# Shifting the matmul activations by 32 bytes and the arena by 96 bytes against the weights in SBUF

## The reference, cut to what matters

```python
# first block, layer 0 ("a" stages) and layer 1 ("m" stages)
hn = rms_norm(x, norm_mix[i]);  mix = even_mixer(...) or odd_mixer(...)   # @ w_in, attention, @ w_out
x = x + mix
x = x + sqrelu_mlp(rms_norm(x, norm_mlp[i]), mlp_w1[i], mlp_w2[i])        # 1024 -> 4096 -> 1024
# second block ("r" stages, then "f" stages)
proj = rms_norm_2(x) @ w_in                       # 1024 -> 7698: RNN branch, q, k, v, gates
merged = sigmoid(g_a) * (y_a @ w_proj_a) + sigmoid(g_b) * (y_b @ w_proj_b)
x = x + rms_norm_2(merged @ w_out)
up = causal_dwconv(rms_norm_2(x) @ w_up)          # 1024 -> 6144
x = x + rms_norm_2((gelu(gate) * val) @ w_down)   # 3072 -> 1024
```

## Time and profile before

| what | value |
|---|---|
| three timed runs | 1129.11, 1130.38, 1136.15 us (median 1130.38) |
| the profiled execution | 1134.4 us, its span 1132.6 us |
| TensorE matmul busy | 98% of the span |
| VectorE, ScalarE, GpSimd busy | 69%, 52%, 12% |
| mean granted TensorE clock | 0.995 |

### The profile page before, as it was taken

The page is one execution under the profiler, slowest core; times in us unless marked ns, Lnnn a source line. Parts: engine busy times, 40 slices in busy tenths (PEclk is TensorE's granted clock), DMA queues, the critical chain, the costliest instruction groups (busy, mean ns, idle before and its releaser), DMA issues.

```text
span 1132.6 us, 21593 instructions
## 1 busy us (share of the span) xinstructions
PE 1109.1 (98%) x9351; PEld 1068.6 (94%) x9351; DVE 786.1 (69%) x1134; ACT 587.8 (52%) x828; POOL 140.6 (12%) x109
## 2 busy tenths in 40 slices
PE   7999899999999999999999999999999989999998
PEld 6988799999999999999999997999988989999998
DVE  6567488784457566977644689786475889888752
ACT  4477655443336555544433566854366647666531
POOL 4200050001230005000122206201010000111000
PEclk9999999999999999999999999999999999999999
DMA  9943055566654444555555472666464545556551
GB/s 280 276 150 112 1 184 189 186 195 201 200 187 155 154 139 150 186 187 187 186 187 186 132 212 69 200 200 217 131 221 143 188 147 187 186 187 205 186 184 40
DMA packets 195938, 195.72 MB, mean 173 GB/s; under 512 B 9803, under 2 KB 193028, under 8 KB 195844
## 3 DMA queue, kind: packets, MB, share of 16 engines
q1 hardware_dynamic: 193680, 190.53, 52.9%
q10 hardware_dynamic: 2164, 3.82, 1.1%
HBM read 192.86 MB, written 1.47 MB: 172 GB/s over the span
## 4 chain that ended last, share of the span: by engine, by line
PE 94%; DVE 3%; ACT 2%; DMA 0%; issue 0%; DVEq 0%; SPq 0%; ACTq 0%
PE ps_gemm L1727 50%; PE ps_trans L1727 35%; PE ps_score L1804 2%; PE ps_out L1836 2%; PE ps_trans L1821 2%; DVE act_lo L1144 2%; DVE w_lo L1138 1%; PE ps_gemm L1908 1%; PE ps_score L2035 1%; DMA x_in<-in_x 0%; PE ps_out L2035 0%; PE ps_out L2039 0%; PE ps_score L2039 0%; DVE rs L1150 0%; PE ps_score L1770 0%; ACT prob L798 0%
## 5 line engine op out<-in xcount | busy, mean ns | idle before, releaser
L1138 DVE TENSOR_TENSOR w_lo<-raw,w_hi 128x2048 fp32r<-128x2048 f32 (+2 forms) x179 | 408.2, 2289 | 45.2 <-ACT w_hi L753 45.0
L753 ACT ACTIVATE w_hi<-raw 128x2048 fp32r<-128x2048 f32 (+2 forms) x179 | 332.3, 1863 | 175.2 <-DMA raw<-in_mlp_w 95.3
L1727 PE MATMUL ps_gemm<-act_hi,w_hi 128*128 128x256 f32 (+1 forms) x960 | 267.1, 286 | 4.7 <-ACT act_hi L1064 4.4
L1727 PE MATMUL ps_gemm<-act_hi,w_lo 128*128 128x256 f32 (+1 forms) x960 | 259.9, 282 | 0.0
L1727 PE MATMUL ps_gemm<-act_lo,w_hi 128*128 128x256 f32 (+1 forms) x960 | 254.8, 281 | 0.5 <-DVE act_lo L1144 0.4
L1727 PE MATMUL ps_trans<-act_hi,w_hi 128*128 128x256 f32 x688 | 193.1, 281 | 1.9 <-DVE w_lo L1138 1.9
L1727 PE MATMUL ps_trans<-act_hi,w_lo 128*128 128x256 f32 x688 | 193.0, 281 | 0.0
L1727 PE MATMUL ps_trans<-act_lo,w_hi 128*128 128x256 f32 x688 | 192.9, 280 | 0.0
L1727 PEld LDWEIGHTS ps_gemm<-act_hi,w_hi 128*128 128x128 f32 (+1 forms) x960 | 182.1, 192 | 10.2 <-issue 8.2
L1727 PEld LDWEIGHTS ps_gemm<-act_hi,w_lo 128*128 128x128 f32 (+1 forms) x960 | 178.6, 190 | 0.3
L1727 PEld LDWEIGHTS ps_gemm<-act_lo,w_hi 128*128 128x128 f32 (+1 forms) x960 | 173.7, 186 | 2.1 <-DVE act_lo L1144 0.9
(11 more groups left out here) (379 smaller groups left out, 2238.9 us busy)
## 6 DMA issues: line engine op xcount, KB each, us to landing
raw<-in_mlp_w SPq DMA_DIRECT2D x64, 1024.0 KB, 5.4
raw<-in_w_in SPq DMA_DIRECT2D x30, 1024.0 KB, 5.4
raw<-in_w_up SPq DMA_DIRECT2D x24, 1024.0 KB, 5.2
raw<-in_od_w_in SPq DMA_DIRECT2D x12, 1024.0 KB, 5.1
raw<-in_w_down SPq DMA_DIRECT2D x12, 1024.0 KB, 5.2
raw<-in_ev_w_in SPq DMA_DIRECT2D x9, 1024.0 KB, 8.1
raw<-in_w_proj_a SPq DMA_DIRECT2D x8, 640.0 KB, 4.3
raw<-in_ev_w_out SPq DMA_DIRECT2D x4, 1024.0 KB, 5.1
```

The costliest lines, as they stand in the source:

```text
L753: act.activation(w_hi[:, slot, 0:k, 0:n], raw[:, slot, 0:k, 0:n], ACT.Copy).then_inc(hi_done, 1)
L1138: dve.tensor_tensor(w_lo[:, slot, 0:k, 0:n], raw[:, slot, 0:k, 0:n], w_hi[:, slot, 0:k, 0:n].bitcast(F32), ALU.subtract).then_inc(w_ready, 1)
L1727: ins = pe.matmul(dst, lhs, rhs, start=(first and opens and opening), stop=(last and closes and i + 1 == len(order)), skip_group_check=True)
```

## The change

The bytes between `conv_f` and `act_hi` grow by 32, and those between `tmp0`'s 8 KB and the arena by another 64. So `act_hi`, `act_lo` and the scratch stretch begin 32 bytes further on (at 96 modulo 128), the arena and all in it 96 bytes further on (at 32 modulo 128). `raw`, `w_lo`, `w_hi`, `x` and the small tiles stay. No instruction is added, removed or moved; only addresses differ. The last tile still ends inside the partition (the assertion leaves 832 bytes).

```diff
     fw = place("conv_f", [P, 4, 2 * NH2])
+    top[0] += 32
     act_hi = place("act_hi", [P, NX, T], F32R)
     act_lo = place("act_lo", [P, NX, T], F32R)
     tmp0 = top[0]
-    arena = tmp0 + 8 * K
+    arena = tmp0 + 8 * K + 64
     assert arena + 70 * K <= 229344, arena + 70 * K
```

## The result

The changed kernel takes 1149.37 us (median of four runs, 1147.65 to 1151.06) against 1131.94 us (four runs, 1129.11 to 1136.15): 1.0146 times as long, 95% interval 1.0108 to 1.0183. The profiled execution takes 1151.06 us, its span 1149.3 us, against 1134.4 and 1132.6 us. So the loss to be explained in the trace is 16.7 us of span.

What follows compares the result with a forecast made beforehand. The prediction took TensorE's matmul count times start-to-start distance as the bound. Its VectorE, ScalarE, DMA and TensorE terms summed to 0 against the profiled 1134.4 us; expecting a median amid earlier runs, it forecast 1131 us, range 1112 to 1148.

Steps and rivals of the forecast that it cites:

- What bounds the kernel: Whole kernel: TensorE is busy 98% of the span, so time is the number of matmuls times their start-to-start distance.
- VectorE, ScalarE, DMA, 0 us: Reads and transfers at shifted addresses cost 0 us; bounds 0.3 us for VectorE and DMA, at most 1.1 us for ScalarE.
- TensorE, 0 us: All matmuls: 0 us, since residues 0 and 64 modulo 128 gave the same two cadences for moving and stationary sides.
- The second argument: Weight load doesn't set the matmul cadence: with 16 stationary columns, ten starts lie in 1.14 us, 114 ns apart.
- rival 1: Matmuls: shifting moving against stationary reads stops the slow cadence forming; 20.9 us less, 1113.5 us; chance 0.17.
- The bounds of that term: TensorE: -20.9 us if the slow cadence goes, +16 us if 8,400 matmuls each open one more piece of memory (1.9 ns).
- Rival 2: Matmuls of line 1727: every restart falls into the slow cadence, 4.45 ns each; 15.6 us more, 1150 us; chance 0.12.
- Rival 3: Matmuls: one more memory piece per operand on top of either cadence, up to 1.9 ns each; 1145 us; chance 0.07.
- Rival 4: Some 8,200 matmuls: the excess over 106.7 ns of columns goes altogether, 75 us less; 1059 us; chance 0.03.
- Rival 5: Placement: the change doesn't do what it says; 1131 us; chance 0.01.
- The lottery: Dense matmuls: each run draws its mix of fast and slow cadences anew, so the median should be 1131 us, some 4 either side.
- The 109.2 ns: Skill's rule for 256 columns: columns over 2.4 GHz plus about 2.5 ns; over some 8,200 dense matmuls, 55 us less.

Runs made afterwards that it cites:

- the scan: Kernel before with weight slots (one kernel) or hidden-layer quarters (three) at varied distances (moving less stationary operand's start): single executions, 1150.44, 1140.24, 1135.74, 1140.12 us.
- distance 0: Kernel before with activations and arena 64 bytes on, weights unmoved, so moving and stationary operands start at the same residue: 1166.43 us, ratio 1.0296.
- the run on columns: Against the kernel with distance 0: matmuls in `f_up` load only 96, 64 or 16 of 128 stationary columns; single execution, 1158.96 us.
- distance 112: Against the kernel before: weights 16 bytes on, activations and arena 192, so moving activations start 112 past the weights modulo 256: 1162.09 us, ratio 1.0247.

## Why the prediction was wrong, point by point

The forecast was 1131 us, the result 1149.4 us: above the range's upper end of 1148 and 1.5% slower.

**What bounds the kernel: right.** TensorE's start-to-start distance is the time. The distances from each matmul of `gemm` to the next matmul add up to 1010.4 us after and 993.7 us before, a difference of 16.7 us, the whole change of the span.

**VectorE, ScalarE, DMA, 0 us: right.** Lines 1637 and 1091 stand within 2 ns of the earlier trace rows in their medians, busy times within 1.3 us of the earlier trace rows, and the 1 MB loads of `raw` from `in_w_in` land in 5.5 us and `x_in` in 4.4 us, against 5.4 and 4.3 in the earlier trace rows.

**TensorE, 0 us: the step that failed.** The prediction took 0, "the nearest rows being those where a shift of 64 bytes between the two sides changed nothing". It measured +15.4 us. Those rows compare distances -64 and +64, and the scan shows these to be the two places, half a period apart, where the two cadences of 113.3 and 117.8 ns live. They look alike because of that, and say nothing of -32 and +32. I had seen one value of a variable twice and read it as two values without a difference. The second argument, that the weight load doesn't set the cadence since 16 stationary columns run at 114 ns, rests on one slab: at distance 0 that slab stays at 113.5 ns while all with 128 columns take 120.0, so the number of stationary columns does count. And the same trace held the third level that rival 1's "against" denies: its slab with 24 columns ran at 116.7 ns (the lines stand with the run on columns).

**The bounds of that term** were -20.9 and +16 us, and the measured 15.4 lies inside, close to the upper one; but they were bounds for other mechanisms, and distance 0 went to some 33 us. Near as the 1.9 ns a matmul of the upper bound and the measured 1.88 are, that is luck too: no dense run before showed it. The true upper end could not be had from the trace, which held no dense run at another distance.

**Rival 1 (the slow cadence can't form any more)** named the likeliest mechanism (argued, not shown), moving and stationary reads meeting, and the means, a shift of one against the other. It had the sign wrong: the shift removed both cadences, the fast one too, and the two that came are at 116.7 and 118.3 ns. It had 0.17; its mechanism with a sign left open deserved more.

**Rival 2 (every restart into the slow cadence)** gave 1150 us and the result is 1149.4, but not by its mechanism. It wanted 11.31 per 96 everywhere; the chain has 11.36 and 11.20 and no 11.31. The times agree since 4,944 + 576 matmuls lie 0.5 ns above the slow cadence and 2,880 lie 1.1 ns below it. Its place (the matmul's line) was right; that its time came out is luck.

**Rival 3 (one piece more on top of either cadence)** is out: after the change each stage has one value, not two raised ones. **Rival 4** is out, no run went below 113.3 ns. **Rival 5** is out.

**The lottery: right for the kernel before, wrong for the changed one.** The kernel before ranges from 1123.8 to 1143.6 us over 29 runs and on another chip from 1122.1 to 1147.5 over eleven, and the kernel with all tiles moved by 32 bytes, same distance, has fast and slow in other stages. But the forecast of 1131 us took it that the changed kernel would draw from the same two cadences, and it has neither: its trace shows one value for each distance, and its four runs lie within 3.4 us.

**The 109.2 ns, an estimate for 256 columns by the Trainium skill** (TensorE: Matmul & The Clock Gate, "Wait — 56ns, not 53.3ns?"), and the 55 us that would hang on it: placement stands behind the step from 113.3 to 120.0 ns, but at no distance tried, and not with 16 stationary columns either, did a dense stretch run below 113.3 ns. So the runs bear out none of those 55 us.

**What stays open.** What decides, at distance 64 or 192, into which cadence a stretch falls; nothing tried forced it. What meets what: that the distance of the two starts sets the time is shown, that it does so by the weight load's read meeting the moving read is argued, and the slabs with 24 and 16 columns at distance 112 (120.0 and 116.7 ns) speak against its being the load's length alone. Why the period is 256 bytes. Why the stretches at 112 remember what ran ahead. Most values of the table were each seen in one execution, in slabs that followed another distance, and history may be in them as well.

## What to carry to other kernels

Where dense matmuls bound a kernel and each loads 128 new stationary columns, the start of the moving operand relative to the stationary one is a parameter of the kernel: from 113.3 to 120.0 ns here, 3% of the whole. It was seen for fp32r with 256 moving columns alone. Moving everything together changes nothing; whoever inserts a tile between the two should read the time of a fixed number of matmuls in the chain of a dense stage before and after, and not trust alignment, for the aligned distance 0 was the worst. And two rows that "agree" under a swap of roles bear out an independence only if the swap changes the variable modulo its period.

## What the hardware showed that I had not expected

- Start to start of an fp32r matmul (128 x 128 stationary, 256 moving columns) at the 2.4 GHz level: 120.0 ns at distance 0, 118.3 at -32, 116.7 at +32 and +16, 118.7 at 128, and 113.3 or 117.8 at 64 and 192 (each as seen in the stretches of these runs; 112 gave 114.2 and 120.0); 8 bytes off 64 it is 118.8 to 120.0.
- At distance 0 the excess over 113.3 ns hangs on the number of stationary columns: 6.7 ns with 128, 2.7 with 96, none with 64 or 16. At distance 112 it doesn't go: 120.0 ns with 24 columns.
- The phase of the two cadences often survives a slab of 48 matmuls at another distance (10.88, 11.19, 10.88 us per 96) and sometimes flips over it (11.31, 11.41, 10.91 us).
